# Every SBUF operand at a multiple of 128 bytes: large tensors allocated first, arena pieces rounded to 32 floats

## The reference

```python
z = jnp.einsum('td,thkd->thk', xc, u_sel)
a = (jax.nn.gelu(z.astype(jnp.float32)) * g).astype(xc.dtype)
return jnp.einsum('thk,thkd->td', a, v_sel)
```

## Time and profile before

| | us |
|---|---|
| median of 3 runs | 1361.16 |
| lowest, highest | 1357.58, 1363.65 |
| the profiled execution | 1357.5 |
| its span, first to last instruction | 1356.1 |

### The profile page before, as it was taken

One profiled execution on the slowest core, in us unless ns is written; L12 is line 12 of the kernel. 1 busy time (PEld: TensorE's weight loads), 2 busy tenths in 40 slices (PEclk: granted clock), 3 DMA queues, 4 the chain that ended last, 5 costly groups with the idle time before them and its releaser, 6 DMA issues.

```text
span 1356.1 us, 21959 instructions
## 1 busy us (share of the span) xinstructions
PE 1289.0 (95%) x8283; PEld 1112.7 (82%) x8283; DVE 1064.7 (79%) x2318; ACT 596.8 (44%) x1105; POOL 250.1 (18%) x180
## 2 busy tenths in 40 slices
PE   5889999988999889999999999999999999999997
PEld 5577855685696579999999999999988888888886
DVE  5587896686778689999987888888876666666666
ACT  1444682536334535555544444444443333333332
POOL 0363000550000007689940000000000000000001
PEclk9999999999999999999999999999999999999999
DMA  9877542857577254654454444444565555555552
GB/s 353 299 229 281 210 141 90 300 204 274 186 267 263 94 207 135 202 180 149 152 172 148 141 149 148 148 145 152 171 197 190 187 187 186 187 188 187 188 191 99
DMA packets 92382, 256.82 MB, mean 189 GB/s; under 512 B 9472, under 2 KB 16896, under 8 KB 91904
## 3 DMA queue, kind: packets, MB, share of 16 engines
q1 hardware_dynamic: 59728, 195.91, 43.1%
q10 hardware_dynamic: 32560, 59.66, 12.4%
HBM read 254.47 MB, written 1.06 MB: 188 GB/s over the span
## 4 chain that ended last, share of the span: by engine, by line
PE 60%; DVE 17%; POOL 8%; issue 6%; DMA 5%; ACT 3%; SPq 1%; POOLq 0%; ACTq 0%; DVEq 0%
PE bank L1733 26%; PE bank L1726 21%; PE bank L2005 4%; PE bank L1119 3%; DVE arena L430 2%; PE bank L689 2%; POOL u_lo L1765 2%; DVE arena L966 2%; DMA arena<-in_w_in 2%; POOL v_lo L1765 2%; POOL head_ms L820 2%; DVE u_lo L681 2%; DVE v_lo L681 1%; DMA arena<-in_nsa_w_in 1%; DVE arena L1006 1%
## 5 line engine op out<-in xcount | busy, mean ns | idle before, releaser
L1726 PE MATMUL bank<-h_hi,u_hi 128*128 128x256 f32 x632 | 182.7, 289 | 4.0 <-POOL u_lo L1765 2.9
L1726 PE MATMUL bank<-h_hi,u_lo 128*128 128x256 f32 x632 | 178.7, 283 | 0.0
L1726 PE MATMUL bank<-h_lo,u_hi 128*128 128x256 f32 x632 | 178.7, 283 | 0.0
L1726 PEld LDWEIGHTS bank<-h_hi,u_hi 128*128 128x128 f32 x632 | 121.0, 191 | 4.8 <-POOL u_lo L1765 1.9
L1726 PEld LDWEIGHTS bank<-h_lo,u_hi 128*128 128x128 f32 x632 | 121.1, 192 | 0.0
L2162 POOL TENSOR_SCALAR raw<-raw 128x1024 f32<-128x1024 f32 x1 | 3.0, 2995 | 640.2 <-DMA raw<-in_final_g 640.2
L1726 PEld LDWEIGHTS bank<-h_hi,u_lo 128*128 128x128 f32 x632 | 120.9, 191 | 0.0
L2101 ACT ACTIVATE u_hi<-raw 128x1024 fp32r<-128x1024 f32 x64 | 67.9, 1062 | 109.2 <-PE bank L1733 109.2
L2101 ACT ACTIVATE v_hi<-raw 128x1024 fp32r<-128x1024 f32 x64 | 67.9, 1062 | 106.0 <-PE bank L1733 106.0
L1726 PE MATMUL bank<-h_hi,v_hi 128*128 128x256 f32 x392 | 112.9, 288 | 0.9 <-POOL v_lo L1765 0.9
L1726 PE MATMUL bank<-h_hi,v_lo 128*128 128x256 f32 x392 | 110.8, 283 | 0.0
(11 more groups left out here) (275 smaller groups left out, 3479.7 us busy)
## 6 DMA issues: line engine op xcount, KB each, us to landing
raw<-in_u SPq DMA_DIRECT2D x128, 512.0 KB, 3.5
raw<-in_v SPq DMA_DIRECT2D x128, 512.0 KB, 3.5
arena<-in_ada_t SPq DMA_DIRECT2D x80, 512.0 KB, 5.2
arena<-in_ada_w SPq DMA_DIRECT2D x12, 512.0 KB, 12.1
raw<-in_nsa_w_in ACTq DMA_DIRECT2D x3, 2048.0 KB, 11.7
arena<-in_moba_w_in ACTq DMA_DIRECT2D x3, 2048.0 KB, 13.4
arena<-in_w_in ACTq DMA_DIRECT2D x3, 2048.0 KB, 10.6
arena<-in_w_query ACTq DMA_DIRECT2D x3, 2048.0 KB, 11.5
```

The lines of the kernel that those rows point to most:

```text
L1726: last = pe.matmul(zbank[k].t[:, 0:S], u[:, c, :], h[:, c, :], start=n == 0, stop=n == 3 * DC - 1)
```

## The change

The constant `LINE = 32` (floats, 128 bytes) is new, and `carve` starts each piece at the next multiple of it; `LAYER_ROOM` becomes 18080 to match. The large tensors are allocated in front of the small tables, `raw` and `a_hi`, `a_lo` among them. Each large one is a multiple of 128 bytes long, so each begins at one; the small tables stand behind them at multiples of 32 bytes. No instruction, wait, transfer or order is changed.

```diff
-LAYER_ROOM = 18027
+LINE = 32
+LAYER_ROOM = 18080
...
-        at = top[0]
+        at = -(-top[0] // LINE) * LINE
         top[0] = at + n
...
     x = sb("x_tok", [P, NT, D])
     ident = sb("ident", [P, P])
-    cols = sb("cols", [P, NCOL])
-    rows = sb("rows", [P, NROW])
     causal = sb("causal", [P, S])
     cmp_mask = sb("cmp_mask", [P, NT, CPAD])
     iota_k = sb("iota_k", [P, P])
-    pos_i = sb("pos_i", [P, NT + 1], I32)
-    cosd = sb("cosd", [P, NT + 1, ROT])
-    sind = sb("sind", [P, NT + 1, ROT])
-    silu_c = sb("silu_c", [P, 2, DC])
-    ada = [sb("ada0", [P, 24]), sb("ada1", [P, 24]), sb("ada2", [P, 48])]
     gate_row = [sb(f"gate_row{i}", [P, D]) for i in range(2)]
     ones = sb("ones", [P, P])
-    mod_a = sb("mod_a", [P, DC])
-    stat = sb("stat", [P, 8])
-    pow_half = sb("pow_half", [P, NH])
     hkT = sb("hkT", [P, 3, S])
...
     h_hi, h_lo = sb("h_hi", [P, DC, S], F32R), sb("h_lo", [P, DC, S], F32R)
+    raw_all = sb("raw", [P, 4, D])
+    a_hi, a_lo = ([sb(f"a_{part}{k}", [P, S], F32R) for k in range(2)] for part in ("hi", "lo"))
+    cols = sb("cols", [P, NCOL])
+    rows = sb("rows", [P, NROW])
+    pos_i = sb("pos_i", [P, NT + 1], I32)
+    cosd = sb("cosd", [P, NT + 1, ROT])
+    sind = sb("sind", [P, NT + 1, ROT])
+    silu_c = sb("silu_c", [P, 2, DC])
+    ada = [sb("ada0", [P, 24]), sb("ada1", [P, 24]), sb("ada2", [P, 48])]
+    mod_a = sb("mod_a", [P, DC])
+    stat = sb("stat", [P, 8])
+    pow_half = sb("pow_half", [P, NH])
     layers = ExitStack()
     st.callback(layers.close)
 
-    raw_all = sb("raw", [P, 4, D])
     ring = [raw_all[:].rearrange("p a n -> p (a n)")] + [carve([P, DC * WT], layers) for i in range(RING - 1)]
...
-    a_hi, a_lo = ([sb(f"a_{part}{k}", [P, S], F32R) for k in range(2)] for part in ("hi", "lo"))
```

## The result

The changed kernel takes 1347.53 us (median of 4 runs, 1344.49 to 1348.91), the kernel before 1360.77 (median of 4 runs, 1357.58 to 1363.65). The ratio is 0.990, with a 95% interval of 0.9872 to 0.9929: 13 us faster, with 10 to 17 us inside the interval. I had forecast 1360.7 and given the faster case, rival A with 1350.5 us, a chance of 0.18.

What follows compares the result with a forecast made beforehand. PE was taken to bound the kernel, about half the span being one kind of matmul's pace. With 0 from DVE, ACT, PE and POOL and 0 to -1 from DMA, 1361 less half a microsecond gave 1360.7 us, range 1350 to 1366.

Steps and rivals of the forecast that it cites:

- rival A: Output stage: the stationary operand's start separates 233.3 from 226.7 ns; 10.2 us less, 1350.5 us, chance 0.18.
- What bounds the kernel: Whole kernel: PE busy 95%, 60% of the chain; output stage one piece, 350.25 us for 1500 matmuls.
- The list of where the operands stand: SBUF starts modulo 128 before: slots, h and raw at 64, a at 96, most arena pieces at 44.
- DVE, ACT, POOL, DMA: Other engines and loads: 0 from DVE, ACT and POOL, 0 to 1 us less from DMA.
- Rival B: Carved pieces and loads: a small gain, DVE 1.2 and DMA 2 us, 1358 us, chance 0.12.
- rival C: First 43 expert blocks: POOL's reads meet DVE's, 3250 ns each, 16 us slower, 1377 us, chance 0.07.
- PE in the layers and in the hidden stage: Matmuls there: 0, since L1842 at +44 and L797 at +0 go at 112 and 113 ns.
- PE, output stage: 512-column triples at 0.70 us: bounds 0 and 10.2 us less, taken as 0.
- The argument "for it": Output stage against layers' projections: same form and slots, free bank change, pace constant through 350 us, as an address would make.
- The nine matmuls at 231 ns: Layers' projection, 222.34 to 224.42 us: slow pace with h at +64 too, set against rival A.
- The rule on lines: SBUF page's 16-byte lines: +44 rows touch 33 lines instead of 32; expert stages at line starts gain nothing.
- The sum: Whole kernel: 0 from DVE, ACT, PE and POOL, 0 to -1 from DMA; forecast 1360.7 us.

Runs made afterwards that it cites:

- e14: Kernel after with the rounding in carve undone, so the arena pieces are at +44 again: 1348.03 us, ratio 0.9928 to the kernel before.
- e8: Kernel after with h_hi and h_lo at +32, the padding also pushing a 128 bytes on against the slots: 1351.78 us.
- e12: Kernel after with h_hi and h_lo at +192 to the slots and a kept at distance 0 modulo 256: 1341.51 us.
- e5: Kernel after with the u and v slots, h, raw and a all shifted together to +32: 1347.43 us.
- e13: Kernel before with a_hi and a_lo alone 96 bytes further, at distance 0 to the slots modulo 256: 1348.52 us, ratio 0.9918.
- e4: Kernel after with a_hi and a_lo alone at +32: 1358.5 us.
- e6: Kernel after with a_hi and a_lo alone 128 bytes further: 1357.73 us.
- e15: The kernel of e12 again, timed in several runs: 1341.78 us, ratio 0.9872 to the kernel before.
- e16: Kernel after with h_hi and h_lo at +224 to the slots and a kept at distance 0: 1345.65 us.

## Why the prediction was wrong

**What bounds the kernel: right.** The pace of PE in the output stage was the number that counted, and 10 of the profile's 10.7 us came from it. The list of where the operands stand was right too, but in it I had given each start by itself, modulo 128, and never the difference of two starts in one instruction.

**DVE, ACT, POOL, DMA: right.** All medians and means compared above stayed within 8 ns of what rows of before had shown, and e14 shows that the arena pieces carry nothing that can be measured. Rival B is refuted: the half of the change in `carve` is without effect. POOL (rival C) did not slow down.

**PE in the layers and in the hidden stage: right in time, for an incomplete reason.** These stages run as before, since the distances of their fp32r matmuls were 0 before and are 0 after. That an address has no effect there was false: e8 to e12 change the pace of the hidden stage by the place of `h` alone.

**PE, output stage: the step that failed.** It read: "I take 0: the +44 weights of L1842 load within a 112 ns pace, so a start at +96 should not cost in a 233 ns one." The comparison was not one. In L1842 the stationary `qsT` and the moving `keysT` are 4096 floats apart in the arena, both at +44: their distance is 0 modulo 256. In L797 it is 0 as well, and so it is in the earlier trace rows. Every row that I had set against the output stage had two operands in step; the output stage, with `a` at 96 and the slots at 192 modulo 256, had not (distance 160). The bound that I had worked out, 512 x (0.700 - 0.680) = 10.2 us, was the measured 9.95 us (350.25 - 340.30), and its sign; what I chose was the wrong end of it. The argument "for it" in rival A held word for word: same form, same slots, a bank change without cost, a constant pace. It should have outweighed a comparison across two forms. And plain float32 could not have priced it in any case. Where such a matmul reads a weight tile in `raw` and `hT` in the arena, the distance was 192 before and is 0 after, and the pace is the same. The kernel before:

```profile
460.69 3.70 PE L1119 MATMUL bank<-raw,arena 128*128 128x512 f32 x8
```

The kernel after:

```profile
460.02 3.70 PE L1121 MATMUL bank<-raw,arena 128*128 128x512 f32 x8
```

And e8, where `raw` moves the distance to 128:

```profile
456.69 3.70 PE L1123 MATMUL bank<-raw,arena 128*128 128x512 f32 x8
```

The nine matmuls at 231 ns of the earlier trace rows, which I had set against rival A, are a start after a pause. Before and after the change the projections at distance 0 begin with some spacings of 224 to 236 ns (nine from 222 us on in the kernel before; two from 222 us and eight from 352 us on in the kernel after) and then hold 226 and 227. The output stage of the kernel before never came down to these. Rival A's own mechanism, the start of the stationary operand by itself, is false all the same (e5, e13); its price was right because the change happened to set the distance to 0.

**The rule on lines.** The Trainium skill (SBUF — State Buffer, the table at its head) has 16-byte lines and a penalty for each cross to a new one. No such penalty shows here: `carve`'s +44, off such a line, against +0 costs nothing that can be measured (e14: 1348.03 us against 1347.53). The runs show an effect between places that are all at line starts (+0, +32, +64, +96), of which that table says nothing.

**The sum.** 9.95 us of PE in the output stage, and 0.66 before it (the stage begins at 991.95 in place of 992.61), make 10.6 of the span's 10.7. The 0.66 is within the scatter of that start between kernels with the same layers and hidden stage (991.95 in the kernel after, 993.69 in e4). The medians differ by 13.2, the interval reaches down to 10.

**What stays open.** Why the distance matters is not shown. That a weight load and the moving operand's reads beside it get in each other's way is an idea that fits, but it would not explain why 0 is the best distance for 512 columns and one of the two worst for 256. e6 and e8 have one distance and 348.8 and 350.2 us; that they run in two different patterns is seen, but not what chooses between them. Plain float32 of 512 columns shows no dependence at 0, 128 and 192; for the other plain float32 forms, of fewer columns, no comparison is made here.

## What to carry to other kernels

Where matmuls follow each other without a gap at a pace above their column count, compare the starts of stationary and moving tensor modulo 256 bytes, not each with a round number: one line of padding (e13) did what the whole change did. That holds for fp32r; plain float32 matmuls did not react. Scan the distance for each form, because the best one differs between 512 and 256 columns. And a row of the trace tells about an address only if it differs from the case in the property that counts; with two operands that is their relation too.

## What was not expected of the hardware

- The pace of fp32r matmuls of 512 columns depends on the distance between the starts of their two SBUF operands, modulo 256: 226.9 ns at 0, 229.1 at 192, 232.5 to 234.5 at 32, 64, 96, 128 and 160, and in the layers 233.2 at 224. An equal shift of all of them by 32 bytes changes nothing (340.28 against 340.30 us). Plain float32 matmuls of 512 columns keep their pace (eight records in 3.70 us at 0, 128 and 192).
- Fp32r matmuls of 256 columns are slowest at 0 and 128 (2.87 and 2.88 us for 24, at 840 to 880 us) and go down to 2.74 with the moving operand 192 bytes on. The best distance for 512 columns, 0, is one of the worst here.
- None of the instructions of DVE, ACT and POOL that were compared showed a dependence on its start: DVE's 1024 elements take 1218 to 1226 ns at +0, +44 and +64, ACT's copies 1053 to 1062 and POOL's subtractions 2396 to 2418 at +0 and +64. Loads to +0, +44 and +64 land in 3.3 us at best.
- DVE's table of 128 columns (L1994) takes 0.34 us by itself and about 2.4 us beside a residue subtraction of POOL.
- The 10 us in which PE waited 2.11 us in e15 have a granted clock of 0.83, with 1.00 before and behind, and the wait costs more than its own length (the next block takes 3.43 us in place of 2.83). It need not: e16 waits 1.98 us at the same place, and its clock stays at 1.00.
